# A hybrid decoder block on one Trainium2 core: every second low part of the query, key and value weights is made on GpSimd, the others on VectorE

## The reference

```python
mod = (c_act @ w_ada + b_ada)                 # six rows of scales, shifts, gates
h = rms_norm(x, norm1_g) * (1.0 + sc1) + sh1
proj = h @ w_in                               # 1024 x 1280: q 512 | k 128 | v 128 | u 512
q, k = rope(rms_norm(q, q_norm_g)), rope(rms_norm(k, k_norm_g))
attn_out = sliding_window_sink_attention(q, k, v, attn_sinks)
pool_out = per_group_linear(multiscale_pool(u)) * pool_scale
h_res = x + g1 * (concat([attn_out, pool_out]) @ w_o)
h2 = rms_norm(h_res, norm2_g) * (1.0 + sc2) + sh2
out = h_res + g2 * (square(relu(h2 @ w_mlp_in)) @ w_mlp_out)
```

## Time and profile before

| what | value |
|---|---|
| median of three runs | 980.75 us |
| the profiled execution, its own time | 979.74 us |
| its span, first to last instruction | 978.0 us |
| mean granted TensorE clock | 0.996 of full speed |
| TensorE matmul busy | 922.5 us, 94% of the span |
| VectorE busy | 677.9 us, 69% |
| ScalarE busy | 474.7 us, 49% |
| GpSimd busy | 374.4 us, 38% |

### The profile page before, as it was taken

How to read it: one execution, slowest core, us unless ns; L and a number is a source line. 1 busy time by engine, 2 the same in 40 slices (tenths; PEclk the granted TensorE clock), 3 DMA queues, 4 the chain that set the end, 5 groups by cost and what they waited for, 6 DMA issues and landing times.

```text
span 978.0 us, 12577 instructions
## 1 busy us (share of the span) xinstructions
PE 922.5 (94%) x4381; PEld 763.9 (78%) x4381; DVE 677.9 (69%) x1032; ACT 474.7 (49%) x826; POOL 374.4 (38%) x356
## 2 busy tenths in 40 slices
PE   1898899998999999999999999998999999999998
PEld 1687788776778888788887888886877888888787
DVE  6977888888754587655565545444588656789797
ACT  1745556658464564645544554453344444333341
POOL 8052333335332444988888878830000000000000
PEclk9999999999999999999999999999999999999999
DMA  9851432223322240754465435347998637896673
GB/s 357 323 176 53 129 109 65 74 79 129 108 87 86 87 151 29 240 191 165 162 200 187 160 134 163 139 148 253 344 358 313 217 104 243 292 320 225 213 248 120
DMA packets 92270, 175.53 MB, mean 179 GB/s; under 512 B 9320, under 2 KB 26288, under 8 KB 92208
## 3 DMA queue, kind: packets, MB, share of 16 engines
q1 hardware_dynamic: 92096, 174.70, 53.0%
q10 hardware_dynamic: 112, 0.04, 0.0%
HBM read 136.95 MB, written 37.75 MB: 179 GB/s over the span
## 4 chain that ended last, share of the span: by engine, by line
PE 69%; DVE 12%; ACT 6%; DMA 4%; issue 4%; POOL 3%; SPq 1%; DVEq 0%; ACTq 0%; POOLq 0%
PE psum L1976 22%; PE psum L1978 21%; PE psum L1977 21%; DMA down_raw<-in_w_mlp_out 4%; PE psum L1972 2%; DVE down_operands L1707 2%; ACT probs L778 1%; DVE acc L1153 1%; SPq L618 1%; DVE xh L1227 1%; DVE pT_lo L1269 1%; ACT qT L789 1%; PE psum L2073 1%; ACT hT_hi L724 1%; DVE probs L1294 1%
## 5 line engine op out<-in xcount | busy, mean ns | idle before, releaser
L1976 PE MATMUL psum<-down_operands 128*128 128x512 f32 x448 | 176.0, 393 | 5.9 <-DVE down_operands L1707 5.9
L1063 ACT CAST down_operands<-down_raw 128x1024 fp32r<-128x1024 f32 x96 | 100.9, 1053 | 163.1 <-PE psum L1978 60.4
L1978 PE MATMUL psum<-down_operands 128*128 128x512 f32 x448 | 175.1, 391 | 0.0
L1977 PE MATMUL psum<-down_operands 128*128 128x512 f32 x448 | 174.9, 390 | 0.0
L1707 DVE TENSOR_TENSOR down_operands<-down_raw,down_operands 128x1024 fp32r<-128x1024 f32 x93 | 112.9, 1220 | 29.4 <-ACT down_operands L1063 28.4
L1976 PE MATMUL psum<-h2T,w_operands 128*128 128x512 f32 x272 | 107.5, 395 | 1.8 <-DVE act_quads_a L1653 1.3
L1978 PE MATMUL psum<-h2T,w_operands 128*128 128x512 f32 x272 | 106.0, 390 | 0.0
L1977 PE MATMUL psum<-h2T,w_operands 128*128 128x512 f32 x272 | 105.9, 389 | 0.0
L1976 PEld LDWEIGHTS psum<-down_operands 128*128 128x128 f32 x448 | 84.5, 189 | 26.3 <-DVE down_operands L1707 8.8
L1928 POOL TENSOR_TENSOR w_operands<-raw,w_operands 128x512 fp32r<-128x512 f32 x56 | 83.3, 1488 | 42.1 <-ACT w_operands L1015 42.1
L1978 PEld LDWEIGHTS psum<-down_operands 128*128 128x128 f32 x448 | 84.4, 188 | 17.7
(11 more groups left out here) (247 smaller groups left out, 1931.9 us busy)
## 6 DMA issues: line engine op xcount, KB each, us to landing
down_raw<-in_w_mlp_out SPq DMA_DIRECT2D x160, 256.0 KB, 4.3
down_raw<-act_scratch SPq DMA_DIRECT2D x112, 256.0 KB, 3.3
raw<-in_w_ada SPq DMA_DIRECT2D x32, 512.0 KB, 4.5
raw<-in_w_mlp_in SPq DMA_DIRECT2D x32, 512.0 KB, 4.8
act_scratch<-act_quads_a SPq DMA_DIRECT2D x64, 256.0 KB, 2.1
act_scratch<-act_quads_b SPq DMA_DIRECT2D x48, 256.0 KB, 3.4
slots<-in_w_ada SPq DMA_DIRECT2D x8, 512.0 KB, 10.6
xh<-in_x SPq DMA_DIRECT2D x8, 512.0 KB, 6.0
```

The lines of the kernel that those rows point to most:

```text
L1063: nc.scalar.copy(o[:, 0, :, :], r[:, 0:2, :]).then_inc(op2_hi, 1)
L1976: mm(o, wh, ah, start=first, stop=False, skip_group_check=adds)
L1977: mm(o, wh, al, start=False, stop=False, skip_group_check=adds)
L1978: return mm(o, wl, ah, start=False, stop=last, skip_group_check=adds)
```

## The change

The low parts of the `wqkv` pieces with odd k move to GpSimd's program, behind `root_x(1)`, with a semaphore of their own. VectorE keeps those with even k, at the same places in its program. Whoever waited for `wqkv_lo` (TensorE in the first tile, SyncE before it reloads a buffer) now waits for the semaphore of the engine that makes the piece.

```diff
-        wqkv_hi, wqkv_lo = sem("wqkv_hi"), sem("wqkv_lo")
+        wqkv_hi, wqkv_lo, wqkv_lo_pool = sem("wqkv_hi"), sem("wqkv_lo"), sem("wqkv_lo_pool")
...
+        def wqkv_lo_made(eng, k):
+            eng.wait_ge(wqkv_lo_pool if k % 2 else wqkv_lo, k // 2 + 1)
+
         def freed(eng, n):
...
+            elif kind == "wqkv":
+                wqkv_lo_made(eng, k)
             else:
-                eng.wait_ge({"wu": wu_lo, "wqkv": wqkv_lo}[kind], k + 1)
+                eng.wait_ge(wu_lo, k + 1)
...
             lo_wu(3)
-            for k in range(4):
+            for k in (0, 2):
                 lo_wqkv(k)
             make_h(1, 0)
-            for k in range(4, KD):
+            for k in (4, 6):
                 lo_wqkv(k)
...
             root_x(0)
             root_x(1)
 
+            for k in range(1, KD, 2):
+                a = landed(pool, ("wqkv", k))
+                pool.wait_ge(wqkv_hi, k + 1)
+                g.tensor_tensor(wil[:, k, 0:QKV], a[:, 0:QKV], wih[:, k, 0:QKV].bitcast(F32),
+                                ALU.subtract).then_inc(wqkv_lo_pool, 1)
+
...
                     if t == 0 and not u:
-                        pe.wait_ge(wqkv_lo, k + 1)
+                        wqkv_lo_made(pe, k)
```

## The result

The changed kernel takes 983.82 us (median of 20 runs, 981.13 to 989.18), the kernel before 982.04 in 20 runs beside it (978.37 to 985.34). The ratio is 1.0025, with a 95% interval of 1.0014 to 1.0037: 2.5 us slower (982.04 times 0.0025), between 1.4 and 3.6. That is a slowdown clear of zero and, at its middle, within the 0.3% that I had set as the bound. The forecast was +2.1 us, 982.8 on the median of 980.75.

What follows compares the result with a forecast made beforehand. TensorE, busy 94% of the span, was taken to wait 2.4 us for VectorE's low parts in the first tile's q. Turns with GpSimd delay q's last block by 2.1, all passed through: 980.75 + 2.1 = 982.8 us, range 980.0 to 984.8.

Steps and rivals of the forecast that it cites:

- whether the two engines work side by side: First tile's q projection: VectorE and GpSimd take turns where both read two SBUF operands; +2.1 us, otherwise -0.2.
- A pair of turns: One 128x768 subtraction on each engine: 0.87 on VectorE and 1.65 on GpSimd, 2.52 us, against 1.74 on VectorE alone.
- The queues: SyncE's four `raw` loads end some 2 us later, covered by 15 us; GpSimd's `qk_sums` is not kept waiting: cost nothing.
- The schedule: First tile's low parts: GpSimd's k = 1 first, then alternation; q's last block starts at some 50.15 instead of 48.08, +2.1 us.
- if VectorE gets the first turn: Bound at the first low parts: VectorE is served before GpSimd, then the same count ends at 49.80, +1.8 us.
- the 0.3 us in which nobody is ready: Gap from 47.28 to 47.58, before VectorE's k = 6, whose cast on ScalarE ends at 47.51; adds 0.3 us.
- the prediction's own sum: Eight low parts from 39.72: four pairs of 2.52 are 10.1, plus 0.3 idle, against 8.3 before; 2.1 us later.
- The rival of a delay taken up later by slack: After the first tile, TensorE waits for work independent of it and the 2.1 us disappears: 980.8 us; chance 0.15.
- The clock rival: TensorE's clock falls in the new gaps, at 42 to 54 us or later, costing up to 1.7 more: 984.6 us; chance 0.17.
- The rival's other sign: Anywhere in the kernel: one stretch at a clock of 0.50 more than before would also show that TensorE's clock fell.
- The rival without blocking: First tile's low parts: the 128x768 subtractions run side by side on both engines, -0.2 us, 980.5; chance 0.08.

Runs made afterwards that it cites:

- the reordered one: Kernel before, nothing on GpSimd: VectorE makes all eight low parts in a row, then `make_h(1, 0)`; ScalarE's `hi_h(1, 0)` follows its casts; 981.86 against 982.34 us, ratio 0.9999.

## Why the prediction was right

**The mechanism.** The two engines take turns at one port where both read SBUF, and a piece on GpSimd costs VectorE's stretch more than VectorE would need for it. This was the prediction's step "whether the two engines work side by side", read from the earlier trace rows, and the kernel with four subtractions that nobody waits for shows it apart from a slower engine. The kernels with copies and with memsets show that GpSimd's read is what it takes.

**The terms.** GpSimd's 128x768 alone was put at 1.85: 1.83. A pair of turns was put at 2.52: 2.51 between the ends of GpSimd's pieces. VectorE's alone 0.95 stayed. The queues were right: SyncE's four loads and GpSimd's `qk_sums` cost nothing, the latter moved from 53.23 to 56.40, which is the general shift of 0.72 + 2.44.

**The schedule was off in three places, and the errors partly cancel.** It gave GpSimd's k = 1 the first turn, VectorE had it twice: the bound "if VectorE gets the first turn" (+1.8) was the nearer case in its order, and even it expected alternation from there. `make_h(1, 0)` was thus early (42.17) and not late. VectorE's k = 6 still waited 1.25 us for its cast, until 46.01, but GpSimd held its turn until 46.44, so the 0.3 us in which nobody is ready did not occur. And `lo_h(1, 0)` was put behind k = 7; it was issued at 47.18, ahead of it, and took a turn of 0.6 us from GpSimd. Counted so: GpSimd starts at 42.2, four of its turns of 1.70 are 6.8, and two VectorE pieces of 0.85 and one `lo_h` of 0.60 between them are 2.3, together 51.3 (measured: 51.24), less the 0.72 of this execution 50.5 instead of 50.15. In the prediction's own sum: 0.3 less for the idle time, 0.60 more for the `lo_h`, 0.2 more because four turns took 1.70 and not 1.65: 0.5 more by this count, where 0.4 was measured. So +2.44 and not +2.1. The price of a turn was right and the order of service was not; that the sum came so near is in part luck.

**Did it reach the end?** At the third tile it is 2.45 us, so nothing had taken it up by then, and TensorE is again busy for 16.00 of 16.00 us from 60 to 76, as in the earlier trace rows. The ratio's 2.5 us is about the same number.

```profile
60.00:76.00 16.00, 16.00 (x98) 14.28 (x97) 11.80 (x20) 8.43 (x15) 8.63 (x24) 1.00 0.44 143
```

From the third tile to 117 us the shift stays at 2.45 in the first profile and 2.47 in the second, so no slack took it up there. At the down projection 2.28 us are left in the first and 1.60 in the second. What changes them on the way is the clock. The kernel before has a stretch at 0.50 from 120.90 to 124.30. The changed kernel has one too in its first profile (first line below), and none in its second (second line), which is therefore 0.7 us less late behind it: its shift is 2.48 at ScalarE's operation that starts at 120.65 before, and 1.76 at the one at 129.70.

```profile
124.00:128.00 4.00, 4.00 (x16) 3.51 (x15) 3.52 (x7) 3.35 (x7) 2.17 (x2) 0.57 0.00 0
124.00:128.00 4.00, 3.94 (x27) 3.45 (x26) 3.86 (x9) 3.71 (x9) 2.16 (x2) 1.00 0.00 0
```

Such stretches come and go in the other profiles: the kernel with memsets, which leaves the stretch of the change as it was before, has none there and is 0.44 us ahead at the down projection; the reordered one has a second, from 148 to 152 us (0.59), and there loses what was left of its gain. Each is worth 0.7 us or more. So single executions differ on the way by about as much as half of the change costs, and only the ratio of 20 runs, 1.4 to 3.6 us, tells what the change costs. Whether the change makes one of these falls rarer, and so pays part of its delay back, can't be told from one or two profiles of each kernel. The rival of a delay taken up later by slack has no support. Of the 7.2 us between the two profiled spans, 3.0 are there at the down projection (0.72 + 2.28); the other 4.2 arise in it, where executions of one kernel differ as well: the second profile of the changed kernel has a span of 981.6.

**The clock rival** did not come in 42 to 54 us of the changed kernel: from 43.7 to 47.1 us, where I had counted TensorE busy for 1.6 us, it was busy for 2.27 of 3.40 and the clock stayed at 1.00. In the kernel with copies it was busy for 1.66 in that stretch, in the one with four subtractions for 1.84 of 4.00 from 46 to 50, and both were granted half of the clock after it (0.54 and 0.51). There TensorE waited ahead of three or four row blocks in a row from k = 4 on, here ahead of every second one. The rival's other sign, one slow stretch more than before, did come in the first profile, at 922 to 926 us in the down projection (0.59), but the second profile has one fewer than before, so nothing ties it to the change.

```profile
43.70:47.10 3.40, 2.27 (x9) 1.56 (x10) 2.15 (x2) 3.40 (x7) 3.40 (x3) 1.00 0.43 100
```

**The rival without blocking** (-0.2) is excluded by the kernel with four subtractions. What I hadn't stated is that a gain and a loss need not travel alike: up to the third tile the delay of the last block of q went through whole (2.44 to 2.45), while a gain of 1.28 lost half of itself, because another engine was late next.

## What to carry to other kernels

Before work is moved from VectorE to an idle GpSimd, look at what both read: a subtraction with two SBUF operands on VectorE and a subtraction or a copy on GpSimd, which read SBUF too, go one after the other, so the sum of both is what counts, and here the moved half cost about twice as much on GpSimd. GpSimd's time is free beside VectorE operations that read one operand from PSUM, or for operations that only write. A stretch in which TensorE waits for one engine can also be shortened by the order of that engine's own work (here 1.28 us at q's last block, though no gain in the time is shown); then look for who is late next, since a gain can stop there. And follow a shift of a us or two past the next falls of the clock before you call it won or lost.

## What was not expected

A GpSimd operation that is already waiting can be passed by several VectorE operations in a row: 4.84 us for a subtraction whose turn is 1.27, behind four of VectorE, in the same profile in which the next three alternate strictly. Neither GpSimd's idleness nor the moment of the request explains it alone. A blocked turn cost VectorE 0.62 us for a copy on GpSimd, 1.27 for a subtraction of one tile from itself, some 1.7 for the subtractions of the change, and nothing for a memset.
